# Two transformer blocks on one core: queries and keys of the dilated and latent heads turned in 32x32 blocks and carried through DRAM, and norm weights fetched one at a time

## The reference

```
z = rmsnorm(x, g_pre_mix[l]) @ w_in[l]      # moba q,k,v | fox q,k,v,gate | latents | dilated q,k,v
qa, ka = rope(qa), rope(ka)                  # moba: 4 heads of 64, causal softmax at 256 tokens
c_q = rmsnorm(z_cq, g_mla_q); q_c = c_q @ w_mla_q_up          # latent: 4 heads of 64 + 32 rotary
kv = rmsnorm(z_ckv, g_mla_kv) @ w_mla_kv_up; k_rope = rope(z_kr)
qd, kd = rope(qd), rope(kd)                  # dilated: 4 heads of 64, three window/stride branches
o = softmax(scale * q @ k.T + mask) @ v      # for each kind, head and block of 128 queries
x = x + rmsnorm(concat(o) @ w_out[l], g_post_mix[l])
```

## Time and profile before

| | |
|---|---|
| median of 3 runs | 1782.61 us (1778.89 to 1785.88) |
| the profiled execution | 1780.5 us, of which the span is 1778.8 us |
| busy TensorE (PE) | 1763.0 us, 99% |
| busy VectorE (DVE) | 1188.7 us, 67% |
| busy ScalarE (ACT) | 907.6 us, 51% |
| granted TensorE clock | 1.00 in every stretch of 25 us |
| DMA | 367.68 MB, 207 GB/s over the span |

### The profile page before, as it was taken

The page is one execution under the profiler, slowest core; times in us unless marked ns, Lnnn a source line. Parts: engine busy times, 40 slices in busy tenths (PEclk is TensorE's granted clock), DMA queues, the critical chain, the costliest instruction groups (busy, mean ns, idle before and its releaser), DMA issues.

```text
span 1778.8 us, 22264 instructions
## 1 busy us (share of the span) xinstructions
PE 1763.0 (99%) x8359; PEld 1473.8 (83%) x8359; DVE 1188.7 (67%) x1580; ACT 907.6 (51%) x1382; POOL 92.8 (5%) x209
## 2 busy tenths in 40 slices
PE   8999999999999999999999999999999999999998
PEld 7888888888888888888888888887888888888887
DVE  8867766876755666566686766566666667676664
ACT  6655444666444544445464544454444546454443
POOL 4001000200000010001000100001000100010000
PEclk9999999999999999999999999999999999999999
DMA  8337776643777687766586577758776667557773
GB/s 264 120 118 218 225 224 207 179 132 99 239 228 225 204 254 226 225 213 209 196 258 208 166 236 229 230 182 256 231 230 214 204 201 256 194 170 248 222 220 109
DMA packets 312859, 367.68 MB, mean 207 GB/s; under 512 B 76368, under 2 KB 245872, under 8 KB 312496
## 3 DMA queue, kind: packets, MB, share of 16 engines
q1 hardware_dynamic: 310272, 358.51, 63.8%
q0 software_dynamic: 2176, 7.75, 1.5%
q10 hardware_dynamic: 304, 0.01, 0.0%
HBM read 345.23 MB, written 20.97 MB: 206 GB/s over the span
## 4 chain that ended last, share of the span: by engine, by line
PE 92%; DMA 4%; DVE 3%; issue 0%; SPq 0%; ACT 0%; DVEq 0%; POOLq 0%; POOL 0%; ACTq 0%
PE Dp L1921 17%; PE Dp L1923 17%; PE Dp L1922 17%; PE Tp L1922 6%; PE Tp L1923 6%; PE Tp L1921 6%; PE Gp L1921 6%; PE Gp L1922 6%; PE Gp L1923 6%; DMA Z<-held 2%; DVE wlo L1227 1%; DMA held_piece<-inner 1%; PE Gp L2108 1%; PE Tp L2099 1%; PE Dp L2132 1%; PE Tp L1936 0%
## 5 line engine op out<-in xcount | busy, mean ns | idle before, releaser
L1227 DVE TENSOR_TENSOR wlo<-raw,whi 128x1024 fp32r<-128x1024 f32 (+1 forms) x608 | 711.7, 1208 | 332.5 <-ACT whi L762 331.7
L762 ACT ACTIVATE whi<-raw 128x1024 fp32r<-128x1024 f32 (+1 forms) x608 | 607.6, 1045 | 461.2 <-PE Dp L1923 269.6
L1921 PE MATMUL Dp<-whi,a_hi 128*128 128x512 f32 (+2 forms) x768 | 292.5, 381 | 3.4 <-DVE a_lo L1292 3.0
L1923 PE MATMUL Dp<-whi,a_lo 128*128 128x512 f32 (+2 forms) x768 | 287.5, 374 | 0.0
L1922 PE MATMUL Dp<-wlo,a_hi 128*128 128x512 f32 (+2 forms) x768 | 287.2, 374 | 0.0
L1921 PE MATMUL Dp<-whi,b_hi 128*128 128x512 f32 (+1 forms) x492 | 194.5, 395 | 0.3 <-DVE wlo L1227 0.3
L1923 PE MATMUL Dp<-whi,b_lo 128*128 128x512 f32 (+1 forms) x492 | 191.5, 389 | 0.0
L1922 PE MATMUL Dp<-wlo,b_hi 128*128 128x512 f32 (+1 forms) x492 | 191.3, 389 | 0.0
L1921 PE MATMUL Gp<-whi,a_hi 128*128 128x512 f32 x480 | 186.9, 389 | 2.7 <-DVE wlo L1227 2.7
L1921 PE MATMUL Tp<-whi,a_hi 128*128 128x512 f32 x480 | 186.8, 389 | 0.0
L1923 PE MATMUL Gp<-whi,a_lo 128*128 128x512 f32 x480 | 186.8, 389 | 0.0
(11 more groups left out here) (266 smaller groups left out, 2056.1 us busy)
## 6 DMA issues: line engine op xcount, KB each, us to landing
raw<-in_ffn_w_gate_up SPq DMA_DIRECT2D x176, 512.0 KB, 4.9
raw<-in_w_in SPq DMA_DIRECT2D x132, 512.0 KB, 4.6
raw<-in_ffn_w_down SPq DMA_DIRECT2D x88, 512.0 KB, 4.6
raw<-in_w_gate SPq DMA_DIRECT2D x44, 512.0 KB, 3.8
raw<-in_w_up SPq DMA_DIRECT2D x44, 512.0 KB, 4.9
raw<-in_w_down SPq DMA_DIRECT2D x44, 512.0 KB, 4.5
held<-Z SPq DMA_DIRECT2D x120, 128.0 KB, 2.7
Z<-held SPq DMA_DIRECT2D x120, 128.0 KB, 4.7
```

Of the source, the lines that this page charges most:

```text
L762: return nc.scalar.activation(whi[g % W][0:rows, c0:c0 + n], raw[g % R][0:rows, c0:c0 + n], ACT.Copy).then_inc(hi_done, 1)
L1227: return V.tensor_tensor(wlo[g % W][0:rows, c0:c0 + n], raw[g % R][0:rows, c0:c0 + n], whi[g % W][0:rows, c0:c0 + n].bitcast(F32), ALU.sub ...
L1921: mm(o, hi, wh, start=start, stop=False, skip_group_check=True)
L1923: return mm(o, lo, wh, start=False, stop=stop, skip_group_check=True)
```

## The change

1. Dilated and latent items no longer use `turn_qk`, `q_turned` and `k_turned`; fox and moba items still do. VectorE's new `turn_qk(n, e, l)` transposes inside 32x32 blocks: one instruction of 128x512 for a dilated item (four heads of queries and keys), two of 128x384 for a latent item. SyncE's `store_qk` writes each to DRAM and `fetch_qk` brings it back with blocks exchanged. Six pieces a layer go through two block buffers.
2. `scores` of these items read queries and keys with steps of 4 elements (16 bytes) instead of packed. The dilated heads lie by twos on partitions 0 to 63 and 64 to 127; odd heads go to another PSUM bank than even ones. `mask(D0)` therefore is two instructions of 256 columns instead of one of 512.
3. In the second block each of the three norm weights' loads first waits for a chunk of the first FFN (the 5th, 7th and 9th of 11).
4. The semaphore `tri` is merged into `con` (setup only), and counts of `piece_stored` and `piece_in` get offsets.

```diff
+QK_ORDER = {M0: 0, M1: 1, F0: 2, F1: 3}
+QK_PIECES = [(D0, 0), (L0, 0), (L0, 1), (D1, 0), (L1, 0), (L1, 1)]
...
+        qk_blocks = [Z[:, 3784:4296], Z[:, 6872:7384]]
...
+        def score_q(n, h):
+            kind, t = ITEM[n]
+            if kind == "dil":
+                v = dil_qk(t).rearrange("p (s k) -> p k s", k=4)
+                return v[HD * (h % 2):HD * (h % 2) + HD, h // 2, :]
+            if kind == "mla":
+                return mla_q(t).rearrange("p (s h) -> p h s", h=H)[:, h, :]
...
+            if n == D0:
+                return (T(1) if h % 2 else D(0, 1))[:, P * (h // 2):P * (h // 2) + P]
...
+            def store_qk(l, n, e):
+                i = QK_PIECES.index((n, e))
+                sp.wait_ge(piece_turned, 6 * l + i + 1)
...
+                sp.dma_start(held_qk[i], qk_blocks[i % 2][:, 0:cols]).then_inc(piece_stored[i % 2], 16)
+
+            def fetch_qk(l, n, e):
...
+                sp.wait_ge(piece_stored[i % 2], 16 * (3 * l + i // 2 + 1))
...
+                src = held_qk[i].rearrange("(q c) (b n) -> (c b) q n", q=4, b=b)
+                sp.dma_start(dst.rearrange("p (q n) -> p q n", q=4), src).then_inc(qk_in[n], 16)
...
+                    if g == base1(l) + 10:
+                        store_qk(l, D0, 0)
+                        fetch_qk(l, D0, 0)
+                    if g == base1(l) + 12:
+                        store_qk(l, L0, 0)
+                        store_qk(l, L0, 1)
+                        store_qk(l, D1, 0)
+                        fetch_qk(l, D1, 0)
+                        fetch_qk(l, L0, 0)
+                        fetch_qk(l, L0, 1)
+                    if g == base1(l) + 14:
+                        store_qk(l, L1, 0)
+                        store_qk(l, L1, 1)
+                    if g == base1(l) + 15:
+                        fetch_qk(l, L1, 0)
+                        fetch_qk(l, L1, 1)
...
                 for j, n in enumerate(("ffn1_post_2", "mix_post_2", "ffn2_post_2")):
+
+                    pool.wait_ge(fm[0], NJ * f_21(l) + 2 * j + 5)
                     pool.dma_start(gp[j][:, :], A[n][l].partition_broadcast(P)).then_inc(gains_in[1], 16)
...
+            def turn_qk(n, e, l):
...
+                V.transpose(dst, src).then_inc(piece_turned, 1)
...
                 rotate_dil(0, l)
+                turn_qk(D0, 0, l)
                 mask(M1, l)
...
-                k_turned(D0, l)
...
                 latent_query_rope(0, l)
+                turn_qk(L0, 0, l)
+                turn_qk(L0, 1, l)
...
                 rotate_dil(1, l)
+                turn_qk(D1, 0, l)
                 normalise(M1, l)
```

More of the change, by code:

```diff
@@ L138, with build @@
 T0_ORDER = {M0: 0, D0: 1, L0: 2, F0: 3}
-def build(nc, A, held, held_piece, out):
+QK_ORDER = {M0: 0, M1: 1, F0: 2, F1: 3}
+QK_PIECES = [(D0, 0), (L0, 0), (L0, 1), (D1, 0), (L1, 0), (L1, 1)]
+def build(nc, A, held, held_piece, held_qk, out):
     with ExitStack() as ctx:
@@ L341, in build @@
         fg_dve, fg_act, fg_sum, cum_put = sem("fg_dve"), sem("fg_act"), sem("fg_sum"), sem("cum_put")
+        piece_turned, piece_stored = sem("piece_turned"), two("piece_stored")
+        piece_in = [sem(f"piece_in{i}") for i in range(4)]
+        qk_in = {D0: piece_in[0], D1: piece_in[1], L0: piece_in[2], L1: piece_in[3]}
+        TURNED0, STORED0 = 6 * LAYERS, 16 * 3 * LAYERS
+        IN0 = [16 * LAYERS, 16 * LAYERS, 32 * LAYERS, 32 * LAYERS]
         qk_t, q_out, k_out = sem("qk_t"), sem("q_out"), sem("k_out")
@@ L487, in behind @@
             def behind(g):
+                for l in range(LAYERS):
+                    if g == base1(l) + 10:
[14 more added lines that the diff above has]
+                        fetch_qk(l, L1, 1)
                 for l in range(LAYERS):
@@ L1565, in mask @@
                     dve.wait_ge(p_turned, 12 * l + turned_before(earlier[-1] + 1))
+                if n == D0:
+                    for e in range(2):
+                        bank = (T(1, 256) if e else D(0, 1, 256)).rearrange("p (h s) -> p h s", h=2)
+                        ins = V.scalar_tensor_tensor(out=probs[t][:, 2 * e:2 * e + 2, :],
+                                                     in0=bank, scalar=scale,
+                                                     in1=m[:, S - nk:S].unsqueeze(1).broadcast_to([P, 2, nk]),
+                                                     op0=ALU.mult, op1=ALU.add)
+                    ins.then_inc(masked, 1)
+                    return
                 V.scalar_tensor_tensor(out=probs[t], in0=score_view(n), scalar=scale,
@@ L1595, in inverse @@
                     dve.wait_ge(dil_p, 4 * l + 2 * ITEM[n][1] + 2)
-                V.reciprocal(rec(n), sums(n)).then_inc(recd, 1)
+                if ITEM[n][0] == "dil":
+                    V.reciprocal(rec(n).rearrange("p (h e) -> p e h", e=2), sums(n).rearrange("p (e h) -> p e h", e=2)
+                                 ).then_inc(recd, 1)
+                else:
+                    V.reciprocal(rec(n), sums(n)).then_inc(recd, 1)
             def normalise(n, l):
@@ L2477 @@
     held_piece = [nc.dram_tensor(f"held_piece{i}", (P, 512), F32, kind="Internal").ap() for i in range(2)]
-    build(nc, args, held, held_piece, out)
+    held_qk = [nc.dram_tensor(f"held_qk{i}", (P, 384 if ITEM[n][0] == "mla" else 512), F32, kind="Internal").ap()
+               for i, (n, _) in enumerate(QK_PIECES)]
+    build(nc, args, held, held_piece, held_qk, out)
     r = run_bass_kernel_spmd(nc, [arrays], core_ids=[0])
```

131 lines of the change are left out of this document (84 added, 47 removed).

## The result

The changed kernel takes **1787.31 us** (median of 6 runs, 1784.22 to 1788.33) where the kernel before took 1781.58 beside it (6 runs): a ratio of 1.0031, 95% interval 1.0021 to 1.0041. It is slower, by less than the 0.5% that was called the bound of the measurable. The prediction was 1783 in a range of 1774 to 1792, with "same" the likeliest. The number is near, in part by luck: what it is made of is largely not what was written down. The profiled execution is the shortest of the six, 1784.22 us with a span of 1782.5: +3.7 us over the span of before.

The account below looks back on a forecast made before the run. TensorE, busy 1763.0 of 1778.8 us, was taken to bound the kernel. Twice both trip times (24.6) less 24.3 for removed transposes, slack and norm weights gave +0.3 us on the 1782.6 median: 1783, range 1774 to 1792.

Parts of the forecast that it names:

- Transposes removed: On TensorE, eight groups of query and key transposes over two layers go, 0.87 us each: 7.0 us less.
- D0's trip: D0's store to DRAM and fetch before its scores: TensorE idles 1.3 us, scores come 0.4 us later than before.
- T0: Time from D0 being turned until its fetched tile has landed: 6.3 us, ends 5.0 and 9.1.
- D1's trip: D1's store and fetch, behind a full stretch of VectorE: its scores move by +3.0 us, TensorE waits 2.2.
- T1: Time from D1 being turned until its fetched tile has landed: 6.0 us, ends 5.0 and 9.1.
- What stands behind: After D1: L0's and L1's fetches and weight unit 13 stay hidden; their removed transposes win 1.74 us a layer.
- Norm weights: Three loads in the second block's first FFN, spread out, no longer delay fetches: -3.0 us, ends 0 and -3.0.
- Score products of unchanged length: On TensorE, dilated scores keep their 1.09 and 1.92 us; the sum leaves them so.
- rival of 16-byte steps: Scores of D0, D1, L0 and L1 take twice as long: +12.0 us in two layers, 1795; chance 0.04.
- The halves overlap: Rival: dilated score products on partitions 0 to 63 run beside those on 64 to 127: 1780 us; chance 0.28.
- A: Experiments' theory: 16-byte steps halve the score operands' read rate; for dilated items, partition halves running side by side hide it.
- B: Experiments' rival theory: the trips cost; longer score records come from waiting or the latent items' other data path.

Follow-up runs that it names:

- experiment 3: The changed kernel with its score products issued in head order 0, 2, 1, 3, nothing else; 1786.73 us in one run.
- the kernel through DRAM: The changed kernel with latent keys laid head by head and latent queries in pairs of heads, dilated items still through DRAM; 1780.19 us, ratio 1.0002 to the kernel before.
- experiment 7: The changed kernel with no operand step over 8 bytes and D1 turned ahead of L0; 1777.00 us, ratio 0.9982 to the kernel before.

## Why the prediction was right, and where it was not

- **Transposes removed (-7.0 us)**: held. 64 records less; behind D1, L0's transposes are gone from the chain at the 0.87 us predicted.
- **D0's trip (T0 = 6.3)**: over-estimated. 2.19 + 2.84 and the gap between give 5.1 (5.5 in the second layer), near the lower end (5.0), and TensorE waited 0.4 and 0.8 us instead of 1.3. The assumption of 2.9 for the store because a 1 MB unit is just ahead is what failed: 2.19 is nearly the free transfer's 2.0 of the earlier trace rows. The fetch, at 2.84 instead of 3.4, did the rest.
- **D1's trip**: the mechanism and its place held, in numbers too. D1 was turned 13.35 us after D0's scores' start (13.15 predicted), and T1 was 5.45 (6.0 predicted, lower end 5.0). The scores came 18.85 after D0's (19.15), and the waits were 3.0 us in the two layers together (2.2 predicted for each). The two new waits on VectorE stood where they were said to be, at 0.5 and 0.4 us instead of 0.9 and 0.8.
- **What stands behind**: held. No wait for L0 or L1, no late weights.
- **Norm weights (-3.0)**: held. -3.2 by the ratio of the kernel that does only this.
- **Score products of unchanged length**: this is the step that failed. "The dilated scores take 1.09 and 1.92 us, and the sum leaves them so", and the latent ones were not priced in the forecast at all. They are +3.0 us a layer, +6.0 in all. It was in the rival of 16-byte steps, at 4 in 100, which priced L0 and L1 with D0 and D1 at +12.0; the one row that spoke for it (a block transpose whose strided source cost 1.11 against 0.69) was put down to the transposing. The Trainium skill ("SBUF — State Buffer", on SBUF cachelines) asks for two reads of a 16-byte line for full rate. By that rule, the traces agree on both sides: 8 bytes at 0.94 us, 16 bytes at 1.86 to 1.96. The same passage goes on that 4 float32 can be strided for free; read as a step of 4, these times contradict it.
- **The halves overlap** (28 in 100): it is so. Its own counter-argument, that the second record of a head stands before the next head, is refuted by experiment 3's timeline. The Trainium skill ("TensorEngine Tiling (Array Packing)", Key Properties) says that different tiles of the array can run in parallel, and by that rule the traces agree: pairs start 0.01 to 0.04 us apart, 1.92 goes to 1.06. The two rivals happened together and nearly cancelled for the dilated items, which is the case that the list of rivals did not have: each was priced alone.
- **The clock**: in no step. It cost 0.74 us in the profiled run; what it cost in the others no profile shows.

In all, for the spans: +0.3 predicted; -3.4 from shorter trips (10.5 and 10.65 us a layer instead of 12.3); +6.0 from the latent scores; +0.5 from D1's, 0.27 longer in each layer; +0.7 from the clock; -1.7 because the stretch behind the mixers gave 4.7 and not 3.0. That makes +2.4, against +3.7 measured. The missing 1.3 us lie in small pieces: D0 and D1 turned 0.1 to 0.2 us later than reckoned, scores that begin up to 0.15 us behind the landing, 0.2 at the start; not all of it was taken apart. The forecast was near because errors of opposite sign, longer scores on one side and shorter trips and a larger gain behind the mixers on the other, stood against each other. That was luck: the 6.0 us of the latent scores were in no term of the sum.

As to the theories: A is shown in both halves. B is half true: the trips cost (6.3 us between kernels that ran side by side, clock included), but they do not lengthen the scores. Of the 6.1 us between the two profiled spans, 1.1 lie at the start, ahead of any trip (M0's scores at 33.8 against 32.7 us), and 5.0 in the two layers. The profile of the kernel through DRAM shows there 3.7 as waits for the two fetches (2.7 for D1, 1.0 for D0), 0.8 for the second half of `ups(1)`, about 1.7 in two stretches at half clock (9.00 and 9.05 us from D1's scores to L0's, where the changed kernel at full clock has 8.19) and 0.5 in D1's longer scores, less 3.5 for the transposes saved: 3.2. The rest was not taken apart.

## What to carry to other kernels

When a layout is changed to save an engine's instruction, price the reads of the new layout as well: a float32 operand of TensorE with a 16-byte step cost twice the time when it was streamed and 1.7 times when it was loaded, and one with 8 bytes next to nothing. Two 64-row operands are worth placing on both halves of the partitions, and a 128x128 transpose of two heads at once does it for half the transposes. A wait on an engine that is busy 99% of the time can be paid twice, if the clock falls behind it; and a wait that disappears from the list has gone only if the time fell too.

## What the runs showed of the hardware

- A **16-byte step** in a float32 operand: scores of 256 columns and 64 rows 1.92 to 3.78 us for eight records; weight loads 188 to 327 ns. An 8-byte step (queries): L0's scores 0.94 against 0.89 packed.
- **Products on different halves of the partitions** with a PSUM bank for each half overlap in both orders of issue tried (starts 0.01 to 0.04 us apart), also where the odd heads' records are issued behind all the even ones.
- **A short idle time can bring the clock down.** In the second layer 1.04 us of idle in one 2 us window was followed by about 3.4 us at 1.2 GHz; in the first layer 1.05 us was followed by no fall. With the wait filled with transposes, the clock stayed at 2.4 in both.
- **A stretch at half the clock need not cost half its length.** The 3.4 us at 1.2 GHz cost 0.74 us: the score products with 16-byte steps on both halves took 2.19 us at either clock, while those with 8-byte steps of experiment 7 took 2.08 at the lower, against 1.06 for packed ones at full clock.
- **Slower products are followed by a fall as well.** With the keys' step alone TensorE was busy throughout 50 to 60 us, at a mean granted clock of 0.83:

```profile
50.00:60.00 10.00, 10.00 (x36) 6.84 (x36) 5.19 (x8) 5.62 (x10) 0.00 (x0) 0.83 0.28 101
```

What exactly decides whether the clock falls was not found.
